# A layer norm's second statistics taken from a running sum and from ScalarE's squares, in a hybrid decoder layer

## The reference, cut to what matters

```python
D_MODEL, SEQ, DEC_BATCH = 1024, 512, 8
ALPHA = 2.0 ** 0.25
LN_EPS = 1e-5

def layer_norm(x, w=None, b=None):
    mu = jnp.mean(x, axis=-1, keepdims=True)
    var = jnp.mean(jnp.square(x - mu), axis=-1, keepdims=True)
    y = (x - mu) * lax.rsqrt(var + LN_EPS)
    if w is not None:
        y = y * w + b
    return y

mix, ... = token_mixer(h, ...)                     # ends with merged @ w_out
x  = layer_norm(ALPHA * x + (1.0 + g1) * mix, ln1_w, ln1_b)   # the first norm
h2 = layer_norm(x) * (1.0 + sc2) + sh2                        # the second norm
ff, ... = conv_ffn(h2, ...)                        # begins with h2 @ ffn_up
x  = layer_norm(ALPHA * x + (1.0 + g2) * ff, ln2_w, ln2_b)
```

## Time and profile before

| | |
|---|---|
| median of three runs | 1261.82 us (1259.34, 1261.82, 1265.6) |
| the profiled execution | 1261.48 us, of which the span of the core's work is 1259.7 us |
| busy in the span | PE 90%, DVE 56%, ACT 39%, POOL 8% |
| the stretch 790 to 807 us | PE busy 10.2 of 17.0 us, DVE 15.5, ACT 9.8, POOL 11.6 |
| the stretch 807 to 826 us | PE busy 17.2 of 19.0 us, DVE 16.7, ACT 10.0, POOL 6.0 |
| the stretch 826 to 835 us | PE busy 5.0 of 9.0 us, DVE 4.7, ACT 6.0, POOL 0.0 |

### The profile page before, as it was taken

How to read it: one execution, slowest core, us unless ns; L and a number is a source line. 1 busy time by engine, 2 the same in 40 slices (tenths; PEclk the granted TensorE clock), 3 DMA queues, 4 the chain that set the end, 5 groups by cost and what they waited for, 6 DMA issues and landing times.

```text
span 1259.7 us, 34799 instructions
## 1 busy us (share of the span) xinstructions
PE 1134.9 (90%) x15404; PEld 1035.7 (82%) x15404; DVE 701.6 (56%) x1131; ACT 487.0 (39%) x800; POOL 100.3 (8%) x152
## 2 busy tenths in 40 slices
PE   3858999999999999979999699789999999789995
PEld 1357888888888888879998699689999998789995
DVE  2144665666666765459724344856666666633226
ACT  0335534445345333443333222545353435422221
POOL 0000220211303202000000000500000000000000
PEclk9978999999999999999999899899999999989998
DMA  8330220220210201168765642132323232342321
GB/s 268 131 106 2 56 58 3 59 58 4 58 44 18 73 22 54 36 185 226 209 191 188 197 117 85 50 102 84 94 72 92 75 100 67 113 126 81 92 67 68
DMA packets 185120, 117.50 MB, mean 93 GB/s; under 512 B 6324, under 2 KB 177130, under 8 KB 184705
## 3 DMA queue, kind: packets, MB, share of 16 engines
q1 hardware_dynamic: 154833, 100.37, 26.6%
q10 hardware_dynamic: 30160, 15.21, 4.3%
HBM read 108.40 MB, written 7.34 MB: 92 GB/s over the span
## 4 chain that ended last, share of the span: by engine, by line
PE 30%; DVE 8%; issue 8%; ACT 6%; DMA 2%; SPq 1%; POOL 1%; DVEq 1%; ACTq 0%; POOLq 0%
PE PJ L231 22%; PE PJ L223 4%; ACT Wh L1644 2%; ACT ACC L1838 2%; DVE ACC L2237 2%; DVE ACC L2238 1%; PE BB L1413 1%; DVE ACC L2245 1%; DVE ACC L2243 1%; ACT ACC L1836 1%; DMA RAW<-in_w_branch_rwkv_dram 1%; DVE Wl L1888 1%; DMA RAW<-in_w_in_dram 1%; DMA AD<-in_ada_w_dram 1%; SPq L1324 0%
## 5 line engine op out<-in xcount | busy, mean ns | idle before, releaser
L231 PE MATMUL PJ<-Hh,Wh 128*128 128x260 f32 (+1 forms) x1184 | 266.2, 306 | 38.5 <-DVE Wl L1888 13.3
L231 PE MATMUL PJ<-Hh,Wl 128*128 128x260 f32 (+1 forms) x1184 | 241.3, 285 | 1.4 <-issue 1.4
L231 PE MATMUL PJ<-Hl,Wh 128*128 128x260 f32 (+1 forms) x1184 | 242.5, 287 | 0.0
L231 PEld LDWEIGHTS PJ<-Hh,Wh 128*128 128x128 f32 x1184 | 186.3, 191 | 61.9 <-issue 32.4
L231 PEld LDWEIGHTS PJ<-Hh,Wl 128*128 128x128 f32 x1184 | 186.2, 191 | 1.6 <-issue 1.6
L231 PEld LDWEIGHTS PJ<-Hl,Wh 128*128 128x128 f32 x1184 | 186.6, 192 | 0.0
L1888 DVE TENSOR_TENSOR Wl<-RAW,Wh 128x1024 fp32r<-128x1024 f32 (+2 forms) x102 | 118.2, 1161 | 119.9 <-ACT Wh L1644 114.8
L1644 ACT ACTIVATE Wh<-RAW 128x1024 fp32r<-128x1024 f32 (+2 forms) x106 | 106.8, 1010 | 138.3 <-PE PJ L231 116.3
L2237 DVE SCALAR_TENSOR_TENSOR ACC<-ACC,CP 128x512 f32<-128x512 f32 x88 | 66.0, 750 | 71.6 <-ACT ACC L1838 70.0
L1207 POOL TENSOR_TENSOR MO<-BP,CST 128x512 f32<-128x512 f32 x40 | 55.8, 1401 | 312.1 <-DVE KP L1085 251.6
L231 PE MATMUL PJ<-SFh,Wh 128*128 128x256 f32 (+1 forms) x308 | 64.7, 292 | 13.4 <-DVE Wl L1888 13.4
(11 more groups left out here) (372 smaller groups left out, 2150.0 us busy)
## 6 DMA issues: line engine op xcount, KB each, us to landing
RAW<-in_w_in_dram SPq DMA_DIRECT2D x46, 512.0 KB, 4.8
RAW<-in_ffn_up_dram SPq DMA_DIRECT2D x44, 512.0 KB, 3.8
AD<-in_ada_w_dram ACTq DMA_DIRECT2D x19, 512.0 KB, 5.6
RAW<-in_ffn_down_dram SPq DMA_DIRECT2D x16, 512.0 KB, 3.9
RAW<-in_ada_w_dram ACTq DMA_DIRECT2D x10, 512.0 KB, 5.5
RAW<-in_ada_w_dram SPq DMA_DIRECT2D x2, 2048.0 KB, 10.6
ACC<-in_ada_w_dram SPq DMA_DIRECT2D x2, 2048.0 KB, 13.0
RAW<-in_w_branch_rwkv_dram SPq DMA_DIRECT2D x8, 512.0 KB, 4.6
```

The costliest lines, as they stand in the source:

```text
L231: mm = pe.matmul(out[:, b, 0:nb[b]], w[:, slot, kw, :], x[:, kx, c0:c0 + nb[b]], start=first and w is Wh and x is xh, stop=last and w is Wl)
```

## The change

`finish` of the first norm gets an accumulator output for these five tiles (`finish_x`): besides its result it writes the row's sum. `mean_x` turns the sum into -mean with one small TENSOR_SCALAR. On ScalarE `root_x` first runs Square with -mean as the bias over the row (1024 wide, its elements go into XN, which is overwritten later) and takes the sum of the squares from the accumulator output, then the root, with a scale of 1/1024. `inverse_x` keeps only the reciprocal; -mean/std is made by a small Copy on ScalarE at the head of `normed`. The statistics `stats_x` and the aggregate are gone. ScalarE also runs one small Sqrt on a constant before the branch products (new line 1715), so that the table load stands there. And the orders of ScalarE and VectorE are rewritten around it: `gated1(6)` and `gated1(7)` come after the first and the second XN tile, `split_ff(1)` after the first root, `split_ff(2)` after `gated1(7)`, `split_ff(3)` after the first block of Hh. PE, SP and GpSimd issue what they did, in the same order.

```diff
                 act.wait_ge(S("po_out"), 32)
+                act.activation(BO[:], CST[:, C_EPS:C_EPS + 1], ACT.Sqrt)
                 act.wait_ge(S("out"), 16 * 5)
...
                 def root_x(t, n):
+                    r = ROWS[t]
                     past(act, "mv", n)
-                    act.activation(RS2[0:ROWS[t], t:t + 1], MVX[0:ROWS[t], t, 1:2], ACT.Sqrt,
-                                   bias=CST[0:ROWS[t], C_EPS:C_EPS + 1]).then_inc(S("sd"), 1)
+                    act.activation(xn_row(t), x_row(t), ACT.Square, bias=MVX[0:r, t, 0:1], accum_out=MVX[0:r, t, 1:2]).then_inc(S("sq"), 1)
+                    act.wait_ge(S("sq"), t + 1)
+                    act.activation(RS2[0:r, t:t + 1], MVX[0:r, t, 1:2], ACT.Sqrt, scale=1.0 / D,
+                                   bias=CST[0:r, C_EPS:C_EPS + 1]).then_inc(S("sd"), 1)
 
                 def normed(t, n):
+                    r = ROWS[t]
                     act.wait_ge(S("nb"), n)
+                    act.activation(NB2[0:r, t:t + 1], MVX[0:r, t, 0:1], ACT.Copy, scale=RS2[0:r, t:t + 1]).then_inc(S("nc"), 1)
+                    act.wait_ge(S("nc"), n)
                     act.activation(xn_row(t), x_row(t), ACT.Identity, bias=NB2[0:ROWS[t], t:t + 1],
                                    scale=RS2[0:ROWS[t], t:t + 1]).then_inc(S("xn"), 1)
...
                 gated1(NF + 1)
+                root_x(0, 2)
                 split_ff(1)
-                root_x(0, 2)
+                normed(0, 1)
                 gated1(NF + 2)
-                split_ff(2)
-                gated1(NF + 3)
-                normed(0, 1)
-                split_ff(3)
                 root_x(1, 3)
                 normed(1, 2)
+                gated1(NF + 3)
+                split_ff(2)
...
                     half_h(b, 0)
+                    if b == 0:
+                        split_ff(3)
...
-                def stats_x(t):
+                def finish_x(t):
                     n = ROWS[t]
-                    for b in range(2):
-                        bs = dve.bn_stats(ST2[0:n, t, b, :], x_row(t)[:, 512 * b:512 * b + 512])
-                    need(mark(bs))
-                    dve.bn_aggr(MVX[0:n, t, :], ST2[0:n, t].rearrange("p b s -> p (b s)")).then_inc(S("mv"), 1)
+                    dve.scalar_tensor_tensor(x_row(t), x_row(t), RS1[0:n, t:t + 1], LNP[0:n, 1, :], ALU.mult, ALU.add,
+                                             accum_out=ST2[0:n, t, 0, 0:1]).then_inc(S("x1"), 1)
+
+                def mean_x(t):
+                    n = ROWS[t]
+                    dve.wait_ge(S("x1"), t + 1)
+                    dve.tensor_scalar(MVX[0:n, t, 0:1], ST2[0:n, t, 0, 0:1], -1.0 / D, None, ALU.mult).then_inc(S("mv"), 1)
 
                 def inverse_x(t, n):
 
                     m = ROWS[t]
                     past(dve, "sd", n)
-                    need(mark(dve.reciprocal(RS2[0:m, t:t + 1], RS2[0:m, t:t + 1])))
-                    dve.scalar_tensor_tensor(NB2[0:m, t:t + 1], MVX[0:m, t, 0:1], -1.0, RS2[0:m, t:t + 1], ALU.mult, ALU.mult).then_inc(S("nb"), 1)
+                    dve.reciprocal(RS2[0:m, t:t + 1], RS2[0:m, t:t + 1]).then_inc(S("nb"), 1)
...
                 inverse(0, 2, 1)
                 need(c0)
-                finish(x_row, LNP, 0)
-                dve.wait_ge(S("x1"), 1)
-                stats_x(0)
+                finish_x(0)
                 c1 = centre(x_row, LNP, 1)
+                mean_x(0)
+                need(c1)
+                finish_x(1)
                 gated_s(MO1, NF + 1, 2, PJ[(NF + 1) % 2], KT + 2)
+                mean_x(1)
                 inverse_x(0, 2)
```

More of the change, by code:

```diff
@@ L2140, in _ @@
                 need(c0)
[L2141 to L2143 removed]
+                finish_x(0)
                 c1 = centre(x_row, LNP, 1)
+                mean_x(0)
+                need(c1)
+                finish_x(1)
                 gated_s(MO1, NF + 1, 2, PJ[(NF + 1) % 2], KT + 2)
+                mean_x(1)
                 inverse_x(0, 2)
[L2147 to L2149 removed]
                 gated_s(MO1, NF + 2, 2, PJ[(NF + 2) % 2], KT + 3)
[L2151 removed]
+                inverse_x(1, 3)
                 add(6, XA, XAS, (2, 3), NF, 2, True, B[2])
                 gated_s(MO1, NF + 3, 2, PJ[(NF + 3) % 2], KT + 4)
[L2154 removed]
                 dve.wait_ge(S("xa"), 7)
@@ L2170, in _ @@
                 need(c2)
-                finish(x_row, LNP, 2)
-                dve.wait_ge(S("x1"), 3)
-                stats_x(2)
+                finish_x(2)
                 c3 = centre(x_row, LNP, 3)
-                inverse_x(2, 5)
-                need(c3)
-                finish(x_row, LNP, 3)
-                dve.wait_ge(S("x1"), 4)
-                stats_x(3)
-                c4 = centre(x_row, LNP, 4)
+                mean_x(2)
+                need(c3)
+                finish_x(3)
+                c4 = centre(x_row, LNP, 4)
+                mean_x(3)
+                inverse_x(2, 5)
+                need(c4)
+                finish_x(4)
                 inverse_x(3, 6)
-                need(c4)
-                finish(x_row, LNP, 4)
-                dve.wait_ge(S("x1"), 5)
-                stats_x(4)
+                mean_x(4)
                 HB = [PJ[0][:, 1, :], PJ[1][:, 1, :], B[1], B[3]]
```

5 lines of the change are left out of this document (removed).

## The result

The changed kernel takes 1268.25 us (median of 17 runs, 1265.12 to 1272.96), the kernel before 1260.81 us (17 runs beside them, 1257.39 to 1266.67). The ratio is 1.0061, with an interval of 1.0046 to 1.0076: 7.4 us slower. The profiled execution of it has a span of 1268.9 us.

A forecast was written before the change was run, and what follows sets the result against it. The prediction took the chain of waits to the last Hl, ahead of PE's 78 matmuls, as the bound. 4.2 + 1.3 + 0.3 = 5.8 us on 1261.48 gave 1267.3, median 1267.6; range 1262.5 to 1271.5.

The forecast's parts named there:

- XN's transposes: First half of the norms: PE's transposes of XN start at 805.3 instead of 807.04, a gain of 1.7 us.
- last Wl: GpSimd's last Wl, behind the late split of tile 3, ends at 812.0 us; before, it ended at 805.70.
- one turn of both engines: At the shared port, one VectorE two-tile operation plus one GpSimd Hl takes 2.1 to 2.2 us; 2.2 taken.
- last Hl: Second half: after four turns GpSimd's last Hl ends at 820.8 instead of 816.56, 4.2 us later.
- small Copy ahead of HS: ScalarE's small Copy before the sample rows' XN adds 0.3 us on the chain before PE's second pass.
- The mechanism: Second half: VectorE's two-tile operations and GpSimd's subtractions alternate at one port; the removed statistics had let GpSimd through; 4.2 us.
- The first turn: First half: GpSimd's first Wl gets the port before finish_x(0), which ends at 795.0 instead of 793.43.
- The clock term: PE's clock rises later in the 78 matmuls: 0 to 2.6 us, middle of 1.3 taken.
- Rival 1: GpSimd is served first at the port, last Hl ends before 817; 1261.7 to 1263.1 us, no change; chance 0.17.
- Rival 2: VectorE's finish with accumulator output runs at half rate or as an extra pass: 3 us more, 1270.6; chance 0.12.
- Rival 3: PE's clock stays low through the pass: 2 to 5 us more, 1270 to 1272; chance 0.11 together with Rival 4.
- Rival 4: VectorE's mean_x queues for the port, XN as late as before: 1268 to 1270; chance 0.11 together with Rival 3.

The follow-up runs named there:

- hl_on_dve: The changed kernel with the first half's four Hl made by VectorE instead of GpSimd, splits still late; stage 41.99 us, ratio to before 1.0040.
- spare_stats: The changed kernel with two unused BN_STATS put back on VectorE behind finish_x of tiles 2 and 3; stage 45.43 us, ratio to before 1.0054.
- filler: The changed kernel with useless matmuls on PE, 44 ahead of the first Hl wait and 8 ahead of each other; stage 44.90 us, ratio to before 1.0061.
- early_splits: The changed kernel with ScalarE's splits of tiles 1 to 3 moved earlier; stage 44.93 us, ratio to before 1.0057.
- no_pool_after: The changed kernel with early splits and GpSimd's four Wl and four Hl moved to VectorE; stage 38.97 us, ratio to before 0.9999.
- no_pool_after_filled: The changed kernel with early splits, GpSimd's Wl and Hl on VectorE, and useless matmuls in PE's idle places; stage 40.81 us, ratio to before 0.9999.
- after_padded: The changed kernel with 11 useless one-column memsets on VectorE ahead of the feed-forward loop; loop 254.16 us, ratio to before 1.0047.
- no_early_sqrt: The changed kernel without the small early Sqrt, so the table load is at the first root again; stage 47.44 us, ratio to before 1.0046.

## Why the prediction was right, point by point

The forecast was 1267.6 us, the result 1268.25. Its steps, in us relative to before within the stage:

| step | forecast | measured |
|---|---|---|
| XN's transposes | 1.7 earlier | 2.1 earlier (15.13 against 17.21) |
| last Wl | 6.3 later | 6.0 later |
| one turn of both engines | 2.2 | 2.2 (8.90 / 4) |
| last Hl | 4.2 later | 4.0 later |
| 78 matmuls (clock) | 1.3 longer | 2.3 longer (11.80 against 9.49) |
| small Copy ahead of HS | 0.3 | 0.3 |
| stage | 5.8 | 6.65 |
| feed-forward loop | none | 1.0 |

**The mechanism was right**, and this is the step that carried it: the two engines take turns at one port, and work taken from VectorE, which was not late, was room for GpSimd. hl_on_dve and the two kernels without GpSimd show that the lateness of the last Hl hangs on the port, and spare_stats gives the removed statistics 0.95 us of it. That is less than the forecast made of them ("they are what was removed"): the late splits alone make the last Hl 1.4 us late, 0.65 is a later first Hl, and for the remaining 1.0 the new order of VectorE's operations is argued above and not tested. The first turn came as forecast too: with the table load gone, Wl 0 got the port before `finish_x(0)`.

**The clock term was too small** by 1.0 us. I took the middle between 0 and 2.6, and it came near the upper end. PE's idle time before the first piece had grown from 1.26 to 7.16 us, for which I had the numbers (XN earlier, Hl later) and did not add them up. filler, which takes that idle time away, has the 78 matmuls in 9.4 us.

**The loop was missing**, 1.0 us. No view of before could give its size, and that fewer VectorE instructions ahead of a loop could change the loop was not considered. So a part of the close agreement of the median (0.65 us) is luck: the terms that I had sum to 5.8, the measured to 7.65, and the medians differ by 7.4; the forecast median stood on a before of 1261.8 from three runs, of which 17 runs made 1260.81. The rise was 1.6 us too small and its base 1.0 us too high, and the two errors cancel in part.

**The rivals.** Rival 1 (GpSimd first, last Hl before 817): no, they took turns, and the last Hl ended at 822.6. Rival 2 (half rate): no, 1.28 us. The Trainium skill, "Vector Engine (DVE) Microarchitecture Reference", section "7. Points that are easy to get wrong", says that such an operation with two sources that are not bf16 runs at half throughput. The trace does not agree: 1024 columns of float32 from two tiles take 1.28 us with and without accumulator output. Rival 3 (clock low beyond 826): nearly, since 826 to 828 still had 0.54, at 1.0 us more than taken, below the 2 that it asked. Rival 4 (`mean_x` queues): no, 0.14 us.

**What I had wrong** when I planned the experiments is the blame on the moved splits: I expected them to be worth 5 to 7 us in either direction. They cost 1.8 us by themselves, and moving them back gains 2.1 in the stage, but makes XN late again: each order buys one side's port time with the other's.

**Left open**: by their ratios early_splits and filler are 1.6 and 1.0 us slower than their sums in the table let expect, no_pool_after, no_pool_after_filled and after_padded 1.2 to 1.9 us faster, and no_early_sqrt 2.4. The sums are from one execution each and the intervals reach 2 to 3 us each way, so nothing is to be read from it.

## What to carry to other kernels

Where two engines take turns at a shared resource, ask of each operation that you remove whether it used the resource: an operation that did not was the other engine's turn, and taking it away can slow what the chain waits for. Fold a reduction into a neighbour only after the profile shows that the reducing engine is what is late; with the port free, old and new sums gave the same stage here (38.57 and 38.97 us), since PE turned the earlier result over no earlier. And before you explain a change of a few tenths of a per cent, measure the parts that the change did not touch.
